# Head pairs taken two by two in the first mixer of a macaron encoder

## The chip, the cores and the metric

The kernel runs on one core of a Trainium2 chip. Its engines work side by side, each through its own queue in order: TensorE (PE) multiplies and transposes into PSUM, ScalarE (ACT) copies and exponentiates, VectorE (DVE) adds, subtracts and normalises, GpSimd (POOL) and SyncE (SP) start loads. They meet through semaphores: an instruction waits until a counter has reached a number. The metric is the device time of one call in microseconds (us).

## The reference

Two layers of 256 frames and width 1024, all in float32. Each layer is an FFN, a mixer and an FFN, each followed by a layer norm. The first layer's mixer is chunked attention with a learned bias by distance; with 256 frames every query sees all keys up to the end of its 64-frame chunk.

```python
for i in range(DEPTH):                                   # DEPTH = 2
    h = swiglu(x, ffn_w_gate[i, 0], ffn_w_up[i, 0], ffn_w_down[i, 0])
    x = layer_norm(ALPHA * x + 0.5 * h, ln_g[i, 0], ln_b[i, 0])
    y = chunked_rel_attention(...) if i % 2 == 0 else stick_breaking_attention(...)
    x = layer_norm(ALPHA * x + y, ln_g[i, 1], ln_b[i, 1])
    h = swiglu(x, ffn_w_gate[i, 1], ffn_w_up[i, 1], ffn_w_down[i, 1])
    x = layer_norm(ALPHA * x + 0.5 * h, ln_g[i, 2], ln_b[i, 2])

# chunked_rel_attention, per 64-frame chunk; 16 heads of 64
qkv = x @ w_qkv
s = einsum('bqhd,bkhd->bhqk', q_c, k_c) * scale + bias
p = softmax(where(valid, s, -inf))
out = einsum('bhqk,bkhd->bqhd', p, v_c)
return out @ w_o
```

## The kernel before

Weights stream from memory in units of 128 x 2048 numbers (1 MB). Each is split into a high and a low part: ACT rounds it (`hi_unit`, L651) and DVE subtracts (`lo_unit`, L847). A product in near-float32 accuracy is then three matmuls, high by high, low by high and high by low (`three`, L344 to L346, 512 columns each). In the query-key blocks and the FFN the weights stand in the array instead, and high and low parts of x run past them in 512 and 256 columns (`qk_block`, L524 and L527).

A mixer has 16 units: four for the values, eight for query and key of a head pair (`qk`), four for the output, a group of two pairs each. Heads go in pairs (`pp` 0 to 7), and a pair passes these steps:

- PE: `qk_block` makes query and key, eight k-steps of four matmuls, in one accumulator `QK` that all pairs share. So the next block waits until the sum of the last one is made (`qk_ready`).
- ACT: `qk_copy` (L754) copies one half of the accumulator to `both`; DVE: `qk_add` (L1029) adds the other and writes `qkT[pp % 2]`, which frees the accumulator.
- PE: `scores` (L564), float32 matmuls of 64 rows, the two heads side by side in the array.
- DVE: `soften` (L994) adds the bias and finds the row's top; ACT: `exps` (L762); DVE: `normalise` (L1001, L1006).
- PE: `turn_probs` (L574), six transposes; ACT: `probsT_copy` (L779) to the one buffer `probsT`.
- PE: `head_out` (L586, L587), float32 matmuls with 64 columns of the array, into `HEADOUT`; ACT: `headout_hi_part` (L783), DVE: `headout_lo_part` (L1033) split the result for the output product.

The order on each engine is written by hand. PE runs pair pp + 1's query-key block, a fill (k-steps of the second value half, or blocks of the output product), pair pp - 1's head products, pair pp + 1's scores and pair pp's transposes, without a stop. ACT and DVE have the splits of units between the steps of a pair (`HI_EARLY`, `HI_LATE`, `LO_EARLY`, `LO_LATE`). The fill `FILL_FIRST` of four k-steps (12 matmuls) stands behind block 0; later fills have two or more. The last output group (g = 3) is the one that needs pairs 6 and 7; its first six matmuls read pair 6, the next pair 7. POOL loads the bias of pair pp + 2 once pair pp is softened. A unit's load starts when the unit four before it has been split.

Of the kernel before, what the change touches and what calls it, by code (L numbers as in the profile page):

```python
# [26 lines left out]
P = 128  # L27
# [42 lines left out]
NORM_SCALE = [(2 * ALPHA, 4 * EPS), (ALPHA, EPS), (2 * ALPHA, 4 * EPS)] * DEPTH  # L70


MIX_ORDER = [("v", 0, 0), ("v", 0, 1), ("qk", 0), ("v", 1, 0), ("qk", 1), ("v", 1, 1), ("qk", 2), ("qk", 3),
             ("qk", 4), ("qk", 5), ("o", 0), ("qk", 6), ("o", 1), ("qk", 7), ("o", 2), ("o", 3)]
# [12 lines left out]
MIX_SLOTS = [0, 1, 4, 2, 3, 0, 4, 1, 3, 4, 1, 3, 2, 0, 3, 4]  # L87
SLOT = (FFN_SLOTS + MIX_SLOTS + FFN_SLOTS) * DEPTH
assert len(SLOT) == UNITS and len(FFN_SLOTS) == UNITS_FFN and len(MIX_SLOTS) == UNITS_MIX
assert sorted(RELEASED) == sorted(MIX_ORDER)  # L90
# [12 lines left out]


# [16 lines left out]
def build(nc, x_in, first_in, units, bias, ln_g, ln_b, table, out):  # L121
    with ExitStack() as ctx:
        def sb(name, shape, dt=F32):
            return ctx.enter_context(nc.sbuf_tensor(name, shape, dt))
# [29 lines left out]
        probs = [in_hT(1, f"probs{p}", [P, 2, KEYS]) for p in range(2)]  # L154
        stick = in_hT(1, "stick", [P, 2, KEYS])
        probsT = in_hT(1, "probsT", [P, 2, KEYS])
        gate_act = sb("gate_act", [P, ROWS, CHUNK_F])
        hidden = sb("hidden", [P, ROWS, CHUNK_F])
        both = sb("both", [P, 2, SEQ])
        hiddenT = sb("hiddenT", [P, SEQ])  # L160
        gain = sb("gain", [P, D])
# [156 lines left out]
        def _(pe):  # L318
# [257 lines left out]

            def head_out(m, pp):
                pe.wait_ge(probsT_done, m * PAIRS + pp + 1)
                if m * PAIRS + pp > 0:
                    pe.wait_ge(headout_lo, m * PAIRS + pp)  # L580
                if pp == GROUPS:
                    pe.wait_ge(v_copied, m * 4 + 4)
                for h in range(2):
                    acc = HEADOUT[h * HD:(h + 1) * HD, :]
                    cols = slice((2 * pp + h) * HD, (2 * pp + h + 1) * HD)
                    pe.matmul(acc, v[:, 0, cols], probsT[:, h, 0:2 * P], start=True, stop=False)  # L586
                    last = pe.matmul(acc[:, P:2 * P], v[:, 1, cols], probsT[:, h, 2 * P:3 * P],  # L587
                                     start=False, stop=True)
                last.then_inc(headout_done, 1)

# [3 lines left out]
                else:  # L594
                    out_half(m, *todo[1:])

            def mixer_matmul(m, t, finish):
                v_block(m, 0, 0, range(KD), t, TURN_BETWEEN)
                transpose_x(t, 1, (2,))
                v_block(m, 0, 1, range(KD), t)  # L600
# [24 lines left out]
                finish((2,))  # L625
# [15 lines left out]
        def _(act):  # L641
# [132 lines left out]

            def probsT_copy(m, pp):
                act.wait_ge(probsT_psum, m * PAIRS + pp + 1)
                if m * PAIRS + pp > 0:
                    act.wait_ge(headout_done, m * PAIRS + pp)
                act.activation(probsT[:], SCORES[pp % 2], ACT.Copy).then_inc(probsT_done, 1)  # L779

            def headout_hi_part(m, pp):
                act.wait_ge(headout_done, m * PAIRS + pp + 1)
                act.activation(hT_hi[:, pp, :], HEADOUT, ACT.Copy).then_inc(headout_hi, 1)  # L783

            def mixer_scalar(m, t):
                n0 = MIX_UNIT[m]
                weights = exps if m % 2 == 0 else sigmoids
                hi_unit(n0 + 2)
                xT_hi_part(t, 1)
                copy_v(m, 0, 0)  # L790
                hi_unit(n0 + 3)
                load_table(ACT.Exp if m % 2 == 0 else ACT.Sigmoid)
                copy_v(m, 0, 1)
                hi_unit(n0 + 4)
                hi_unit(n0 + 5)
                qk_copy(m, 0)
# [16 lines left out]
                        headout_hi_part(m, pp - 1)  # L813
                probsT_copy(m, PAIRS - 1)
                headout_hi_part(m, PAIRS - 1)
                load_table(ACT.Silu)

            def xT_first(piece):
# [25 lines left out]
        def _(dve):  # L844
# [179 lines left out]
            def qk_add(m, pp):  # L1024
# [3 lines left out]
                    dve.wait_ge(scores_done, m * PAIRS + pp - 1)  # L1028
                dve.tensor_tensor(qkT[pp % 2][:], QK[:, :, 0:SEQ], both[:], ALU.add).then_inc(qk_ready, 1)  # L1029

            def headout_lo_part(m, pp):
                dve.wait_ge(headout_hi, m * PAIRS + pp + 1)
                dve.tensor_tensor(hT_lo[:, pp, :], HEADOUT, hT_hi[:, pp, :],  # L1033
                                  ALU.subtract).then_inc(headout_lo, 1)

            def mixer_vector(m, t):
                n0 = MIX_UNIT[m]
                norm(t - 1, 1, split_too=True)
                for n in range(n0 + 2, n0 + 6):
# [153 lines left out]
```

## Time and profile before

| | us |
|---|---|
| median of 3 runs | 977.15 (976.37 to 977.27) |
| the profiled execution | 977.04 |
| its span in the trace | 975.3 |
| PE busy | 963.7 (99%) |
| DVE busy | 644.5 (66%) |
| ACT busy | 487.4 (50%) |
| first mixer in the trace | about 186 to 303 |

The span runs from the first to the last instruction in the trace. TensorE's granted clock over the execution is 0.997 of full speed. PE's durations overlap, since a matmul starts before the last one has left the array; what a matmul costs in a stream is the distance between two starts. A row of the timeline merges equal instructions that follow each other: the start of the first, the time from there to the end of the last, and how many.

### The profile page before, as it was taken

Reading aid. Unit: us, or ns where it says so; the run is one execution under the profiler, and the core shown is the slowest. Engines: PE = TensorE matmul, PEld = TensorE weight load, DVE = VectorE, ACT = ScalarE, POOL = GpSimd, SP = SyncE. Lnnn points to the kernel's source line nnn. Section 1 sums busy time; section 2 is a strip of 40 time slices with the busy share of each in tenths; the row PEclk is TensorE's granted clock in tenths of the full one; section 3 lists DMA queues with packets and bytes.
Section 4 is the critical chain, followed back from the end, with each engine's and each line's share of the span. In section 5 each row is a group of like instructions: output and inputs, shape, how many; then the busy total and the mean of one; then the engine's idle time right before and its main releaser. Section 6 shows DMA issues by size and latency. Waiting matters only on the chain.

```text
span 975.3 us, 13323 instructions
## 1 busy us (share of the span) xinstructions
PE 963.7 (99%) x5184; PEld 810.9 (83%) x5184; DVE 644.5 (66%) x764; ACT 487.4 (50%) x605; POOL 41.5 (4%) x71
## 2 busy tenths in 40 slices
PE   8999999999999999999999999999999999999996
PEld 7888888887878888888888888888878788888885
DVE  6666674777567666664676666638777777666635
ACT  6555562366663555562245555443655445555530
POOL 0200000010101000000000000001112100000000
PEclk9999999999999999999999999999999999999998
DMA  9855556475452755557555555653744445555611
GB/s 355 309 177 194 192 194 244 166 238 180 157 173 96 240 182 185 201 179 253 173 175 190 196 176 200 237 193 129 259 145 154 149 149 197 182 201 178 230 73 44
DMA packets 51116, 183.91 MB, mean 189 GB/s; under 512 B 5856, under 2 KB 6144, under 8 KB 51072
## 3 DMA queue, kind: packets, MB, share of 16 engines
q1 hardware_dynamic: 48368, 175.00, 52.5%
q0 software_dynamic: 2560, 8.18, 2.6%
q8 instruction: 29, 0.48, 0.2%
q10 hardware_dynamic: 144, 0.13, 0.0%
q14 instruction: 15, 0.12, 0.0%
HBM read 182.21 MB, written 1.07 MB: 188 GB/s over the span
## 4 chain that ended last, share of the span: by engine, by line
PE 96%; DMA 1%; DVE 1%; issue 1%; ACT 0%; SPq 0%; POOLq 0%; POOL 0%
PE psum L392 31%; PE psum L396 15%; PE psum L344 12%; PE psum L345 12%; PE psum L346 12%; PE psum L524 6%; PE psum L527 3%; PE psum L564 1%; PE psum L574 1%; DMA raw<-in_units 1%; PE psum L332 1%; PE psum L586 1%; PE psum L587 0%; DVE w_lo L847 0%; SPq L292 0%
## 5 line engine op out<-in xcount | busy, mean ns | idle before, releaser
L847 DVE TENSOR_TENSOR w_lo<-raw,w_hi 128x2048 fp32r<-128x2048 f32 x162 | 369.2, 2291 | 193.9 <-ACT w_hi L651 193.7
L392 PE MATMUL psum<-xT,w_hi 128*128 128x512 f32 x1280 | 402.3, 396 | 0.2 <-DVE both L871 0.2
L651 ACT ACTIVATE w_hi<-raw 128x2048 fp32r<-128x2048 f32 x162 | 307.2, 1908 | 89.7 <-PE psum L346 88.6
L396 PEld LDWEIGHTS psum<-xT,w_lo 128*128 128x128 f32 x1280 | 240.5, 188 | 56.8
L396 PE MATMUL psum<-xT,w_lo 128*128 128x256 f32 x1280 | 251.5, 278 | 0.0
L392 PEld LDWEIGHTS psum<-xT,w_hi 128*128 128x128 f32 x1280 | 195.1, 189 | 0.6 <-DVE both L871 0.4
L344 PE MATMUL psum<-w_hi,hT_hi 128*128 128x512 f32 x416 | 163.3, 393 | 0.0
L345 PE MATMUL psum<-w_lo,hT_hi 128*128 128x512 f32 x416 | 162.0, 389 | 0.0
L346 PE MATMUL psum<-w_hi,hT_lo 128*128 128x512 f32 x416 | 162.0, 389 | 0.0
L694 ACT ACTIVATE hT_hi<-hiddenT 128x256 f32 (+1 forms) x82 | 34.2, 418 | 203.1 <-DVE hiddenT L876 203.1
L346 PEld LDWEIGHTS psum<-w_hi,hT_lo 128*128 128x128 f32 x416 | 78.1, 188 | 16.5
L344 PEld LDWEIGHTS psum<-w_hi,hT_hi 128*128 128x128 f32 x416 | 78.1, 188 | 15.9 <-issue 0.3
L345 PEld LDWEIGHTS psum<-w_lo,hT_hi 128*128 128x128 f32 x416 | 78.2, 188 | 15.3
L524 PE MATMUL psum<-xT,w_hi 128*128 128x512 f32 x256 | 81.5, 399 | 0.0
L881 DVE TENSOR_TENSOR hT_lo<-hiddenT,hT_hi 128x256 f32 (+1 forms) x82 | 34.9, 426 | 54.9 <-ACT hT_hi L694 54.9
L871 DVE TENSOR_TENSOR both<-psum,both 128x512 f32<-128x512 f32 x82 | 56.7, 692 | 8.5 <-ACT both L684 6.8
L527 PEld LDWEIGHTS psum<-xT,w_lo 128*128 128x128 f32 x256 | 48.1, 188 | 11.3
L684 ACT ACTIVATE both<-psum 128x512 f32<-128x512 f32 x82 | 48.9, 596 | 10.7 <-PE psum L396 10.1
L701 ACT ACTIVATE xT<-psum 128x256 fp32r<-128x256 f32 (+1 forms) x30 | 13.1, 455 | 80.2 <-PE psum L332 80.2
L527 PE MATMUL psum<-xT,w_lo 128*128 128x256 f32 x256 | 50.4, 278 | 0.0
L344 PE MATMUL psum<-w_hi,xT 128*128 128x512 f32 x112 | 45.3, 405 | 0.0
L345 PE MATMUL psum<-w_lo,xT 128*128 128x512 f32 x112 | 43.8, 391 | 0.0
(78 smaller groups left out, 642.6 us busy)
## 6 DMA issues: line engine op xcount, KB each, us to landing
raw<-in_units SPq DMA_DIRECT2D x324, 512.0 KB, 4.7
gain<-in_ln_g POOLq DMA_DIRECT2D x6, 512.0 KB, 3.9
shift<-in_ln_b POOLq DMA_DIRECT2D x6, 512.0 KB, 5.0
first<-in_first SPq DMA_DIRECT2D x2, 768.0 KB, 8.8
first<-in_first SPq DMA_DIRECT2D x3, 384.0 KB, 6.2
x<-in_x SPq DMA_DIRECT2D x1, 1024.0 KB, 17.2
rel<-bias_by_distance POOLq DMA_DIRECT2D x8, 128.0 KB, 4.6
out<-x SPq DMA_DIRECT2D x4, 256.0 KB, 2.0
```

The costliest lines, as they stand in the source:

```text
L344: pe.matmul(acc, st[0], mv[0], start=first, stop=False)
L345: pe.matmul(acc, st[0], mv[1], start=False, stop=False)
L346: return pe.matmul(acc, st[1], mv[0], start=False, stop=last)
L392: pe.matmul(TILE[j][:, which, :], as_gu(w_hi[s])[:, k, at:at + P], xT[:, kk, :, :], start=kk == 0, stop=False)
L396: last = pe.matmul(TILE[j][:, which, 0:SEQ], as_gu(w_lo[s])[:, k, at:at + P], xT[:, kk, 0, :], start=False, stop=kk == KD - 1)
L524: pe.matmul(QK[:, which, :], hi[:, k, which * P:(which + 1) * P], xT[:, k, :, :], start=k == 0, stop=False)
L527: last = pe.matmul(QK[:, which, 0:SEQ], lo[:, k, which * P:(which + 1) * P], xT[:, k, 0, :], start=False, stop=k == KD - 1)
L651: act.activation(w_hi[slot][:], raw[raw_slot][:], ACT.Copy).then_inc(hi_done, 1)
L684: act.activation(both[:], TILE[j][:, :, SEQ:], ACT.Copy).then_inc(small_copied, 1)
L847: dve.tensor_tensor(w_lo[slot][:], raw[raw_slot][:], w_hi[slot][:], ALU.subtract).then_inc(lo_done, 1)
L871: dve.tensor_tensor(both[:], TILE[j][:, :, 0:SEQ], both[:], ALU.add).then_inc(summed, 1)
L881: dve.tensor_tensor(hT_lo[:, at, :], hiddenT[:].rearrange("p (k n) -> p k n", k=1), hT_hi[:, at, :], ALU.subtract).then_inc(hT_lo_done, 1)
```

## The change

In the first mixer alone (`DOUBLE = (0,)`) the pairs go two by two. Query-key blocks 2c + 2 and 2c + 3 come with a fill between them, then the transposes of pairs 2c and 2c + 1 together, a fill, the head products of both, and behind these the scores of the next two. The head products of an odd pair have a buffer of their own in PSUM, beside the even pair's, and `probsT` has a second buffer, in the room of the FFN's `gate_act` and `hidden`. High and low parts of two pairs are then made by one 512-column operation on ACT and one on DVE, released for both at once. ACT and DVE follow the same order, written out in `weights_by_two` and `pairs_by_two`. The order of the mixer's weight units and their slots have a table for each mixer; in the first one the last value unit stands one place later and the output units stand behind all query-key units. On DVE the low part of the last unit moves behind the norm. The second mixer keeps its order and its waits, with `probsT` and `HEADOUT` in two buffers.

```diff
+BEFORE_PAIRS = [[("v", 0, (0, 1))], [("v", 0, (2, 3))]]
+BETWEEN_QK = [[("v", 0, (4, 5, 6, 7))], [("v", 1, (3, 4))], [("o", 0, 0, 0)]]
+BEHIND_TURN = [[("v", 1, (0, 1, 2))], [("v", 1, (5, 6, 7))], [("o", 1, 0, 0)]]
+LAST_PAIRS = [[("o", 0, 0, 1), ("o", 0, 1, 0), ("o", 1, 0, 1), ("o", 2, 0, 0)], [("o", 2, 0, 1)], [("o", 0, 1, 1)]]
...
+DOUBLE = (0,)
...
+        probsT = [probsT, nc.alloc_sbuf_tensor_at("probsT1", [P, 2, KEYS], F32, offset=gate_at)]
...
-        HEADOUT = psum[:, 4, 0:SEQ]
+        HEADOUTS = psum[:, 4, :].rearrange("p (k n) -> p k n", k=2)
+        HEADOUT = [psum[:, 4, p * SEQ:(p + 1) * SEQ] for p in range(2)]
...
             def head_out(m, pp):
                 pe.wait_ge(probsT_done, m * PAIRS + pp + 1)
-                if m * PAIRS + pp > 0:
+                if m * PAIRS + pp > 0 and not (m in DOUBLE and pp % 2 == 1):
                     pe.wait_ge(headout_lo, m * PAIRS + pp)
...
+            def pairs_by_two(m):
+                for pp in range(2):
+                    qk_block(m, pp)
+                    for todo in BEFORE_PAIRS[pp]:
+                        fill(m, todo)
+                for pp in range(2):
+                    scores(m, pp)
+                for c in range(PAIRS // 2 - 1):
+                    qk_block(m, 2 * c + 2)
+                    for todo in BETWEEN_QK[c]:
+                        fill(m, todo)
+                    qk_block(m, 2 * c + 3)
+                    for pp in (2 * c, 2 * c + 1):
+                        turn_probs(m, pp)
+                    for todo in BEHIND_TURN[c]:
+                        fill(m, todo)
+                    for pp in (2 * c, 2 * c + 1):
+                        head_out(m, pp)
+                    for pp in (2 * c + 2, 2 * c + 3):
+                        scores(m, pp)
+                for todo in LAST_PAIRS[0]:
+                    fill(m, todo)
+                turn_probs(m, PAIRS - 2)
+                for todo in LAST_PAIRS[1]:
+                    fill(m, todo)
+                turn_probs(m, PAIRS - 1)
+                for todo in LAST_PAIRS[2]:
+                    fill(m, todo)
+                for pp in (PAIRS - 2, PAIRS - 1):
+                    head_out(m, pp)
+
+            def mixer_matmul(m, t, finish):
+                v_block(m, 0, 0, range(KD), t, TURN_BETWEEN)
+                transpose_x(t, 1, (2,))
+                v_block(m, 0, 1, range(KD), t)
+                (pairs_by_two if m in DOUBLE else pairs_by_one)(m)
...
-                if m * PAIRS + pp > 0:
-                    act.wait_ge(headout_done, m * PAIRS + pp)
-                act.activation(probsT[:], SCORES[pp % 2], ACT.Copy).then_inc(probsT_done, 1)
+                if m * PAIRS + pp > 1:
+                    act.wait_ge(headout_done, m * PAIRS + pp - 1)
+                act.activation(probsT[pp % 2][:], SCORES[pp % 2], ACT.Copy).then_inc(probsT_done, 1)
+
+            def headout_hi_two(m, pp):
+                act.wait_ge(headout_done, m * PAIRS + pp + 2)
+                act.activation(hT_hi[:, pp:pp + 2, :], HEADOUTS, ACT.Copy).then_inc(headout_hi, 2)
...
+            def headout_lo_two(m, pp):
+                dve.wait_ge(headout_hi, m * PAIRS + pp + 2)
+                dve.tensor_tensor(hT_lo[:, pp:pp + 2, :], HEADOUTS, hT_hi[:, pp:pp + 2, :],
+                                  ALU.subtract).then_inc(headout_lo, 2)
...
                 norm(t, 0)
+                if m in DOUBLE:
+                    lo_unit(n0 + 17)
```

PE before, from the end of a fill over pair 1's head products to the block behind them (L586 and L587 are `head_out`, L564 `scores`, L574 `turn_probs`, L524 `qk_block`; probsT_56 is the buffer, qkT0 and qkT1 are those of even and odd pairs):

```order
L346 MATMUL psum<-w_hi2,xT 128x512
L586 MATMUL psum<-probsT_56,v_52 64x256
L587 MATMUL psum<-probsT_56,v_52 64x128
L586 MATMUL psum<-probsT_56,v_52 64x256
L587 MATMUL psum<-probsT_56,v_52 64x128
L564 MATMUL psum<-qkT1_51 128x128 x2
L564 MATMUL psum<-qkT1_51 128x256 x2
L574 MATMUL psum<-ident,probs0_53 128x128 x6
L524 MATMUL psum<-xT,w_hi3 128x512 x2
```

PE now, at the first such place (L598 and L599 are `head_out`, L576 `scores`, L536 `qk_block`):

```order
L358 MATMUL psum<-w_hi2,xT 128x512
L598 MATMUL psum<-probsT_56,v_52 64x256
L599 MATMUL psum<-probsT_56,v_52 64x128
L598 MATMUL psum<-probsT_56,v_52 64x256
L599 MATMUL psum<-probsT_56,v_52 64x128
L598 MATMUL psum<-probsT1_57,v_52 64x256
L599 MATMUL psum<-probsT1_57,v_52 64x128
L598 MATMUL psum<-probsT1_57,v_52 64x256
L599 MATMUL psum<-probsT1_57,v_52 64x128
L576 MATMUL psum<-qkT0_50 128x128 x2
L576 MATMUL psum<-qkT0_50 128x256 x2
L576 MATMUL psum<-qkT1_51 128x128 x2
```

Two pairs' head products and two pairs' scores stand together, and no transposes follow them; those (L586 now) stand ahead of a fill.

ACT before, from the copy of the last quarter of the values on (L747 values, L783 high part of head products, L779 `probsT_copy`, L762 `exps`, L651 split, L754 `qk_copy`):

```order
L747 ACTIVATE v_52<-psum 128x512
L783 ACTIVATE hT_hi<-psum 128x256
L779 ACTIVATE probsT_56<-psum 128x768
L762 ACTIVATE probs1_54,total<-probs1_54,neg_top 128x128
L762 ACTIVATE probs1_54,total<-probs1_54,neg_top 128x256
L762 ACTIVATE probs1_54,total<-probs1_54,neg_top 128x128
L762 ACTIVATE probs1_54,total<-probs1_54,neg_top 128x256
L651 ACTIVATE w_hi0<-raw2 128x2048
L754 ACTIVATE both<-psum 128x512
```

ACT now, from the same copy on (L793 values, L697 split, L829 high part of head products, L808 `exps`, L800 `qk_copy` of block 6):

```order
L793 ACTIVATE v_52<-psum 128x512
L697 ACTIVATE w_hi0<-raw0 128x2048
L697 ACTIVATE w_hi1<-raw1 128x2048
L829 ACTIVATE hT_hi<-psum 128x512
L808 ACTIVATE probs0_53,total<-probs0_53,neg_top 128x128
L808 ACTIVATE probs0_53,total<-probs0_53,neg_top 128x256
L808 ACTIVATE probs0_53,total<-probs0_53,neg_top 128x128
L808 ACTIVATE probs0_53,total<-probs0_53,neg_top 128x256
L800 ACTIVATE both<-psum 128x512
```

Two splits of units stand now between the values and the head products' high part, and the copy of the query-key block stands behind one pair's exponentials and ahead of the other's.

DVE before, at the mixer's end (L847 split, L1033 low part of head products, then the norm of the first 128 frames, L904 to L928, and L889, the low part of the transposed x):

```order
L847 TENSOR_TENSOR w_lo0<-raw1,w_hi0 128x2048
L1033 TENSOR_TENSOR hT_lo<-psum,hT_hi 128x256
L847 TENSOR_TENSOR w_lo1<-raw2,w_hi1 128x2048
L1033 TENSOR_TENSOR hT_lo<-psum,hT_hi 128x256
L904 SCALAR_TENSOR_TENSOR x<-x,psum 128x512
L908 BN_STATS stats<-x 128x6
L904 SCALAR_TENSOR_TENSOR x<-x,psum 128x512
```

DVE now, behind the low parts of pairs 6 and 7 (one operation, L1132) and one split: the norm (L1003 to L1027), L946 the split, L988 the low part of the transposed x:

```order
L1003 SCALAR_TENSOR_TENSOR x<-x,psum 128x512
L1007 BN_STATS stats<-x 128x6
L1003 SCALAR_TENSOR_TENSOR x<-x,psum 128x512
L1007 BN_STATS stats<-x 128x6
L1011 BN_AGGR mean_var<-stats 128x2
L1013 TENSOR_SCALAR var_eps<-mean_var 128x1
L1019 SCALAR_TENSOR_TENSOR x<-x,mean_var,gain 128x256 x2
L1027 SCALAR_TENSOR_TENSOR x<-x,rstd,shift 128x256 x2
L1019 SCALAR_TENSOR_TENSOR x<-x,mean_var,gain 128x512
L1027 SCALAR_TENSOR_TENSOR x<-x,rstd,shift 128x512
L946 TENSOR_TENSOR w_lo1<-raw2,w_hi1 128x2048
L988 TENSOR_TENSOR xT<-psum,xT 128x2x128 x2
```

The split of the last unit (w_lo1) stood between the low parts of pairs 6 and 7, and stands now behind the norm, ahead of the transposed x.

## Rows read from the trace of the kernel before

**Rows 1.** The page, part 4: the chain of waits by engine and line.
```profile
PE 96%; DMA 1%; DVE 1%; issue 1%; ACT 0%; SPq 0%; POOLq 0%; POOL 0%
```

**Rows 2.** Timeline of PE (start us, us, engine line op out<-in), values blocks.
```profile
199.75 0.40 PE L344 MATMUL psum<-w_hi,xT 128*128 128x512 f32 x1
204.30 0.39 PE L346 MATMUL psum<-w_hi,xT 128*128 128x512 f32 x1
```

**Rows 3.** Timeline of PE, one visit, from the fill to the next block.
```profile
238.76 0.39 PE L346 MATMUL psum<-w_hi,xT 128*128 128x512 f32 x1
239.07 0.66 PE L586 MATMUL psum<-probsT,v 128*64 128x256 f32 x4
...
241.91 0.28 PE L527 MATMUL psum<-xT,w_lo 128*128 128x256 f32 x1
```

**Rows 4.** Timeline of PE and its weight loads in narrow windows inside that visit.
```profile
239.34 0.39 PE L586 MATMUL psum<-probsT,v 128*64 128x256 f32 x2
...
239.34 0.15 PEld L587 LDWEIGHTS psum<-probsT,v 128*64 128x64 f32 x2
...
239.67 0.29 PE L587 MATMUL psum<-probsT,v 128*64 128x128 f32 x2
...
240.09 0.50 PE L564 MATMUL psum<-qkT 64*128 64x128 f32 x4
...
240.43 0.38 PE L564 MATMUL psum<-qkT 64*128 64x256 f32 x2
...
240.90 0.38 PE L574 MATMUL psum<-ident,probs 128*128 128x128 f32 x2
...
241.34 0.27 PE L574 MATMUL psum<-ident,probs 128*128 128x128 f32 x1
```

**Rows 5.** Timeline of PE, pair 0's scores between two blocks.
```profile
212.60 0.39 PE L346 MATMUL psum<-w_hi,xT 128*128 128x512 f32 x1
...
214.34 0.40 PE L527 MATMUL psum<-xT,w_lo 128*128 128x256 f32 x2
```

**Rows 6.** Timeline of PE behind query-key block 0, and of DVE there.
```profile
210.09 0.40 PE L344 MATMUL psum<-w_hi,xT 128*128 128x512 f32 x1
...
207.16 4.50 DVE L847 TENSOR_TENSOR w_lo<-raw,w_hi 128x2048 fp32r<-128x2048 f32 x2 [2.19 <-ACT w_hi L651]
211.57 0.68 DVE L1029 TENSOR_TENSOR qkT<-psum,both 128x512 f32<-128x512 f32 x1
```

**Rows 7.** Timeline of PE before pair 1's scores.
```profile
220.60 0.39 PE L346 MATMUL psum<-w_hi,xT 128*128 128x512 f32 x1
221.03 0.93 PE L564 MATMUL psum<-qkT 64*128 64x128 f32 x8
```

**Rows 8.** Timelines of PE, ACT and DVE: the sum of query-key block 1.
```profile
219.22 0.39 PE L527 MATMUL psum<-xT,w_lo 128*128 128x256 f32 x2
...
219.65 0.60 ACT L754 ACTIVATE both<-psum 128x512 f32<-128x512 f32 x1 [0.71 <-PE psum L527]
...
220.28 0.69 DVE L1029 TENSOR_TENSOR qkT<-psum,both 128x512 f32<-128x512 f32 x1 [1.90 <-ACT both L754]
```

**Rows 9.** Timelines of DVE and ACT: softening, exponentials and the split behind them.
```profile
214.94 0.28 DVE L994 CUSTOM_DVE_ANT_0 probs<-psum,rel 128x128 f32<-128x128 f32 x1
...
215.26 0.40 ACT L762 ACTIVATE probs<-probs,neg_top 128x128 f32<-128x128 f32 x1 [2.57 <-DVE neg_top L994]
...
217.04 1.90 ACT L651 ACTIVATE w_hi<-raw 128x2048 fp32r<-128x2048 f32 x1
```

**Rows 10.** Timelines of PE and ACT behind the last head products.
```profile
290.92 0.40 PE L587 MATMUL psum<-probsT,v 128*64 128x128 f32 x4
291.25 0.50 PE L344 MATMUL psum<-w_hi,hT_hi 128*128 128x512 f32 x1
...
291.38 0.39 ACT L783 ACTIVATE hT_hi<-psum 128x256 fp32r<-128x256 f32 x1 [1.39 <-PE psum L587]
```

**Rows 11.** Timeline of DVE behind the first norm of the mixer's end.
```profile
301.78 0.76 DVE L889 TENSOR_TENSOR xT<-psum,xT 128x256 fp32r<-128x256 f32 x2 [1.78 <-ACT xT L701]
```

More of the change, by code:

```diff
@@ L86 @@
 FFN_SLOTS = [j % 4 for j in range(24)] + [4, 0, 1, 2, 3, 0, 4, 2, 3]
[L87 to L90, printed above, removed]
+DOUBLE = (0,)
+MIX_SLOTS = [[0, 1, 4, 2, 3, 0, 3, 4, 1, 0, 4, 0, 1, 2, 3, 4], [0, 1, 4, 2, 3, 0, 4, 1, 3, 4, 1, 3, 2, 0, 3, 4]]
+SLOT = [slot for m in range(DEPTH) for part in (FFN_SLOTS, MIX_SLOTS[m], FFN_SLOTS) for slot in part]
+assert len(SLOT) == UNITS and len(FFN_SLOTS) == UNITS_FFN
+assert all(sorted(RELEASED) == sorted(order) and len(order) == UNITS_MIX for order in MIX_ORDERS)
 def mix_unit(m, *unit):
-    return MIX_UNIT[m] + MIX_ORDER.index(unit)
+    return MIX_UNIT[m] + MIX_ORDERS[m].index(unit)
 def uses_done(n):
-    for at in MIX_UNIT:
+    for m, at in enumerate(MIX_UNIT):
         if at <= n < at + UNITS_MIX:
-            return at + RELEASED.index(MIX_ORDER[n - at]) + 1
+            return at + RELEASED.index(MIX_ORDERS[m][n - at]) + 1
     return n + 1
@@ L595, in fill, with pairs_by_one @@
                     out_half(m, *todo[1:])
[L597 to L600, printed above, removed]
+            def pairs_by_one(m):
                 qk_block(m, 0)
@@ L815, in mixer_scalar, with weights_by_two @@
                 headout_hi_part(m, PAIRS - 1)
+            def weights_by_two(m, n0):
+                hi_unit(n0 + 4)
+                hi_unit(n0 + 5)
+                qk_copy(m, 0)
+                qk_copy(m, 1)
+                hi_unit(n0 + 6)
+                hi_unit(n0 + 7)
+                exps(m, 0)
+                qk_copy(m, 2)
+                exps(m, 1)
+                hi_unit(n0 + 8)
+                copy_v(m, 1, 0)
+                hi_unit(n0 + 9)
+                qk_copy(m, 3)
+                probsT_copy(m, 0)
+                probsT_copy(m, 1)
+                hi_unit(n0 + 10)
+                headout_hi_two(m, 0)
+                exps(m, 2)
+                qk_copy(m, 4)
+                exps(m, 3)
+                qk_copy(m, 5)
+                probsT_copy(m, 2)
+                probsT_copy(m, 3)
+                copy_v(m, 1, 1)
+                hi_unit(n0 + 11)
+                hi_unit(n0 + 12)
+                headout_hi_two(m, 2)
+                exps(m, 4)
+                qk_copy(m, 6)
+                exps(m, 5)
+                hi_unit(n0 + 13)
+                hi_unit(n0 + 14)
+                qk_copy(m, 7)
+                probsT_copy(m, 4)
+                probsT_copy(m, 5)
+                hi_unit(n0 + 15)
+                headout_hi_two(m, 4)
+                exps(m, 6)
+                exps(m, 7)
+                probsT_copy(m, 6)
+                probsT_copy(m, 7)
+                hi_unit(n0 + 16)
+                headout_hi_two(m, 6)
+                hi_unit(n0 + 17)
+            def mixer_scalar(m, t):
+                n0 = MIX_UNIT[m]
+                hi_unit(n0 + 2)
+                xT_hi_part(t, 1)
+                copy_v(m, 0, 0)
+                hi_unit(n0 + 3)
+                load_table(ACT.Exp if m % 2 == 0 else ACT.Sigmoid)
+                copy_v(m, 0, 1)
+                (weights_by_two if m in DOUBLE else weights_by_one)(m, n0)
                 load_table(ACT.Silu)
@@ L1059, in mixer_vector, with pairs_by_two @@
                 headout_lo_part(m, PAIRS - 1)
+            def pairs_by_two(m, n0):
+                qk_add(m, 0)
+                qk_add(m, 1)
+                lo_unit(n0 + 6)
+                soften(m, 0)
+                soften(m, 1)
+                lo_unit(n0 + 7)
+                qk_add(m, 2)
+                normalise(m, 0)
+                normalise(m, 1)
+                lo_unit(n0 + 8)
+                lo_unit(n0 + 9)
+                qk_add(m, 3)
+                lo_unit(n0 + 10)
+                headout_lo_two(m, 0)
+                soften(m, 2)
+                soften(m, 3)
+                qk_add(m, 4)
+                normalise(m, 2)
+                normalise(m, 3)
+                qk_add(m, 5)
+                lo_unit(n0 + 11)
+                lo_unit(n0 + 12)
+                headout_lo_two(m, 2)
+                soften(m, 4)
+                soften(m, 5)
+                qk_add(m, 6)
+                normalise(m, 4)
+                normalise(m, 5)
+                lo_unit(n0 + 13)
+                qk_add(m, 7)
+                lo_unit(n0 + 14)
+                soften(m, 6)
+                headout_lo_two(m, 4)
+                soften(m, 7)
+                normalise(m, 6)
+                normalise(m, 7)
+                lo_unit(n0 + 15)
+                headout_lo_two(m, 6)
+                lo_unit(n0 + 16)
+            def mixer_vector(m, t):
+                n0 = MIX_UNIT[m]
+                norm(t - 1, 1, split_too=True)
+                for n in range(n0 + 2, n0 + 6):
+                    lo_unit(n)
+                (pairs_by_two if m in DOUBLE else pairs_by_one)(m, n0)
                 norm(t, 0)
+                if m in DOUBLE:
+                    lo_unit(n0 + 17)
             def xT_first(piece):
@@ L1164, in mixer @@
         made = []
-        for unit in MIX_ORDER:
+        for unit in MIX_ORDERS[m]:
             if unit[0] == "v":
```

30 lines of the change are left out of this document (10 added, 20 removed), and 4 rows, old and new, of the table MIX_ORDERS.

## The prediction

> **What bounds the kernel now.** I read the page's chain of waits first: TensorE (PE) holds 96% of the way to the last instruction [rows 1]. So only what lengthens or shortens PE's own sequence moves the time, and the question is where PE loses time inside the first mixer (roughly 186 to 303 us). For that I read PE's timeline there by start times, because the durations overlap: of matmuls in one stream only the distance from start to start counts.
>
> In the plain stream a 512-column matmul starts every (204.30 - 199.75) / 20 = 0.2275 us [rows 2]. A query-key block lasts from 204.53 (0.23 after the last row of that stream) to 210.09, that is 5.56 us [rows 2, 6]. Call this full-array stream R, the four head products of a pair H (64 columns of the array), its scores S (64 rows), its transposes T. Inside H one 256-column and one 128-column step together take 239.67 - 239.34 = 0.33, so a pair's H costs 0.65; inside S the same two take 240.43 - 240.09 = 0.34, so S costs 0.66 to 0.68 (I take 0.66); transposes follow each other by (241.34 - 240.90) / 4 = 0.11, so T costs 0.65 [rows 4]. These contents stay. What is on top of them are changes from one kind to another [rows 3, 4]:
> - R to H: 0.31 instead of 0.23 up to the first H, then 0.27 instead of 0.22 to the second: 0.13 in all.
> - H to S: 239.67 to 240.09 is 0.42 where two 128-column steps are 0.22: 0.20.
> - S to T: from the last score to the second transpose, 240.43 to 240.90, is 0.47 against 0.22 + 0.11: 0.14; about 0.05 of it lies behind the first T. T to R: 241.34 to 241.91 is 0.57, against 0.11 + 0.46: 0.01 at most.
> - The whole visit R-H-S-T-R, 238.76 to 241.91, is 3.15, contents 0.23 + 0.65 + 0.66 + 0.65 + 0.46 = 2.65: 0.50 on top.
> - R-S-R, 212.60 to 214.34, is 1.74 with contents of 1.35: 0.39 on top [rows 5]. Entering S costs 0.08 + 0.10, so S to R is 0.21.
>
> **The change part by part.** Before, the mixer makes one R-S-R visit (0.39), one R-S-T-R (0.18 + 0.14 + 0.01 = 0.33), six R-H-S-T-R (3.00), one R-H-T-R (0.13 + 0.10 + 0.05 + 0.01 = 0.29) and a last R-H-R. After, there is one R-SS-R (0.39), three times T T inside R (0.06 each: the slow first transpose and the exit) and R-HH-SS-R (0.13 + 0.20 + 0.21 = 0.54), two single T inside R (0.12) and the same last R-H-R, with two pairs in it. That is 4.01 against 0.39 + 1.80 + 0.12 = 2.31: **1.70 saved**. The trace has no H behind H of another pair, no S behind S and no T straight out of R. I take H behind H and S behind S at nothing, as the steps inside a block. Bounds: if each second block pays its entry again without the change of kind (0.05 for four H, 0.10 for four S) the saving is 1.10; if T out of R is free, it is 2.0. Also one wait goes: before pair 1's scores the gap is 0.43 instead of 0.31 [rows 7], 0.12, because only six matmuls stand between the query-key block and its scores; now pair 0's scores stand between too. **Total saved 1.82.**
>
> Here the page TensorEngine Tiling (Array Packing) of the Trainium skill, section Key Properties, has a rule: changing the tiling mode drains TensorE, changing the tile within a mode does not. The trace agrees with it where the kind changes (0.08 to 0.10 before the first matmul), but shows as much again behind it; by the page's part alone 26 changes become 13, about 0.095 each, and the saving would be 1.2 instead of 1.70.
>
> The other side is what the new order puts between a query-key block and the next one. The next block overwrites the accumulator, so it needs the sum of the former (ACT copies, DVE adds). From the last pair of that block's matmuls (219.22) over ACT (219.65) and DVE (220.28) to the released matmul (221.03) it takes 1.81 [rows 7, 8]; ACT to DVE is 0.63, DVE to PE 0.75. Before, the blocks were separated by two fills, scores and transposes or more. Now:
> - **Block 1 behind block 0.** Two k-steps of values stand between, six matmuls, 1.37, so PE is there at 210.09 + 1.37 = 211.46 by the clock of the trace. DVE's sum, which is in the same place of its queue as before (behind two splits of weights), starts at 211.57 and releases 0.75 later, at 212.32 [rows 6]: **0.86**. With DVE free it would be 0.21 (1.81 - 0.23 - 1.37). Behind PE's wait only PE's own blocks stand.
> - **Block 5 behind block 4.** Six matmuls again, queues clear: 1.81 - 0.23 - 1.37 = **0.21**.
> - **Block 7 behind block 6.** Six matmuls of the first output unit. Here ACT and DVE come late, as both units' splits stand ahead. From the last matmul of the second value half (time 0): ACT's copy of values starts at 0.42 (the 512-column matmul's 0.39 and 0.03); an operation overlaps the next by about 0.1 (on DVE 4.50 for two splits whose steps are 4.41 / 2 = 2.205 [rows 6]), so at 0.92 follows the first split of 1.90 [rows 9], done at 2.82; DVE splits two units in 4.41 until 7.26, subtracts the two head products (0.69 less 0.08, as for the same size in [rows 8]), softens; the exponentials start 0.32 behind that (214.94 to 215.26), at 8.19, and the four take 217.04 - 215.26 = 1.78 [rows 9]; then copy and sum, 0.63 + 0.75: 11.35. PE, from the same 0: 0.23 + 0.13 + 1.30 (HH) + 0.20 + 1.32 (SS) + 0.21 + 5.56 + 1.37 = 10.32. **1.03**, with bounds 0.21 (queues clear) and 1.4.
> - Block 3 has twelve matmuls ahead, 2.73 against 1.81 - 0.23: no wait. Blocks 2, 4 and 6 come behind SS, long after their sums.
> - **Output behind the last heads.** The last group needs pair 6's low part, which was made long before; now pairs 6 and 7 are copied and subtracted together behind pair 7's products. From 290.92 ACT starts at 291.38, 0.46 later; then 0.63 and 0.75 for 512 columns, 1.84; PE would be there at 291.25, 0.33 [rows 10]: **1.51**. The six matmuls that covered pair 7's copy before now stand behind it.
> - Four restarts of R with the weights not yet loaded: a weight load with a wait is not drawn ahead. Of the 0.21 from S to R some 0.09 is the change itself (as from R to H), and 0.11 the first weights of R; in pure R the trace has no such restart. I take 0.08 each, 0.3, bounds 0 and 0.45.
> - **Start of the next FFN.** The last weight unit's low split moves behind the first norm on DVE. It takes 2.21 where DVE was idle for 1.78 [rows 11], so the transposed x comes 0.43 later; PE's slack there is small. I take 0.3, bounds 0 and 0.45.
>
> The sum: -1.82 + 0.86 + 0.21 + 1.03 + 1.51 + 0.3 + 0.3 = **+2.39**. The DMA loads keep their number and size; each is started by a split four units earlier, and a late split is what the sum has already. The second mixer keeps its order and its waits; it only gets second buffers that nothing waited for. The profiled execution took 977.04 (span 975.3 and 1.7 around it), 0.1 below the median of 977.15; the forecast is 977.04 + 2.4 = **979.4**.
>
> **Rivals.**
> A, not slower: ACT and DVE aren't behind. If the splits stand elsewhere when PE arrives, the waits of blocks 1 and 7 are the bare chain, 0.21 each, and the FFN's term vanishes: 2.39 - 0.65 - 0.82 - 0.3 = +0.6, 977.6, within the bound. It decides at a block 1 wait of some 0.5. For it: ACT has free time elsewhere, 1.39 before 291.38 [rows 10]; against it: DVE's start at 211.57 is a row, and nothing ahead of it moves.
> B, slower still: the second blocks pay for their weights. A load of weights for array rows in use would have to wait for the running matmul, so HH and SS cost 0.05 and 0.10 more, four times each: +0.6, 980.0. Against it: in H the next weights load from 239.34 while the matmuls of that start run [rows 4], and the step stays 0.22. The rule is in the Trainium skill's page TensorE: Matmul & The Clock Gate, section The mechanism: loads overlap running matmuls only where the row group differs; by that row this trace does not bear it out for H, whose row groups are the same.
> C, faster: the copies are hidden in some way that I don't see, and only the saving stays: 977.04 - 1.82 = 975.2. Against it: 1.51 at the end rests on a semaphore that counts both pairs.
> D, the backlog spreads: ACT's later start at one group delays the next one's transposes, another 1 us or more, 981.
>
> **How the numbers follow.** Forecast 0.60, A 0.17, B 0.12, C 0.05, D 0.06. A measurement of this kernel tells about 0.2%, 1.95 us, from no change. Slower than that: B, D and most of the forecast (its terms must lose 0.45 to miss it), 0.70. Same: 0.23, A and the rest. Faster: 0.07. The range, 977.5 to 980.7, takes in A and B; below it lies C, above it D.
>
> **What would show it.** In the profile after: L586 (transposes), L598 and L576 in three groups of twelve transposes and of doubled H and S, with starts inside HH and SS at the same steps; PE gaps in front of a query-key block (L536) of about 0.9, 0.2 and 1.0 us, and of 1.5 in front of L356 near the mixer's end. I would be wrong if the first of these gaps is missing, if the gap behind the last heads is much under 1 us, or if HH costs more than 1.4.

## The result, and the profile after

The changed kernel takes 979.35 us (979.01 to 980.14, 10 runs); the kernel before, on the same chip, takes 976.75 (976.25 to 977.28, 10 runs). The ratio is 1.0027, 95% interval 1.0018 to 1.0036: slower, by 2.6 us. The forecast was 979.4, which is 2.4 over the 977.04 of the one profiled execution before. The profiled execution has a span of 977.6 against 975.3.

The chain of waits of the page (part 4) is the first thing to read. Against [rows 1] PE has lost 2 points of it; DVE and ACT have one more each:

```profile
PE 94%; DVE 2%; issue 1%; DMA 1%; ACT 1%; SPq 0%; POOLq 0%; POOL 0%; DVEq 0%; ACTq 0%
```

PE's waits (line <- what released it: total, times, longest) name two causes that the kernel before doesn't have, the accumulator's sum (qkT) and the low part of the head products (hT_lo). The list's other rows are waits in the first 21 us of the program. They differ from trace to trace, and block 0 starts between 203.75 and 204.53 in the nine traces here, so I compare PE from query-key block 0 on.

```profile
PE psum L356 <- DVE hT_lo L1132: 1.6, 1, 1.6
PE psum L536 <- DVE qkT L1128: 1.6, 2, 0.8
```

How much the mixer costs is the distance on PE from block 0's first matmul to one matmul behind the mixer that both kernels have, a k-step of the FFN. After, in two windows of PE's timeline:

```profile
204.22 0.62 PE L536 MATMUL psum<-xT,w_hi 128*128 128x512 f32 x2
...
308.48 0.40 PE L357 MATMUL psum<-w_lo,xT 128*128 128x512 f32 x1
```

And before, the same two instructions:

```profile
204.53 0.62 PE L524 MATMUL psum<-xT,w_hi 128*128 128x512 f32 x2
...
306.22 0.40 PE L345 MATMUL psum<-w_lo,xT 128*128 128x512 f32 x1
```

That is 104.26 against 101.69: **the mixer is 2.57 longer**, and from there to the last matmul the distance between the two kernels doesn't change, the second mixer included. The experiments are read by the same distance.

**The visits**, against [rows 3]. PE's timeline around one double group, with the double transposes of another behind it:

```profile
237.87 0.39 PE L358 MATMUL psum<-w_hi,xT 128*128 128x512 f32 x1
238.19 0.66 PE L598 MATMUL psum<-probsT,v 128*64 128x256 f32 x4
238.67 0.40 PE L599 MATMUL psum<-probsT,v 128*64 128x128 f32 x4
238.89 0.65 PE L598 MATMUL psum<-probsT,v 128*64 128x256 f32 x4
239.32 0.44 PE L599 MATMUL psum<-probsT,v 128*64 128x128 f32 x4
239.69 1.58 PE L576 MATMUL psum<-qkT 64*128 64x128 f32 x16
241.20 0.72 PE L536 MATMUL psum<-xT,w_hi 128*128 128x512 f32 x2
241.76 0.40 PE L539 MATMUL psum<-xT,w_lo 128*128 128x256 f32 x2
...
254.20 1.48 PE L586 MATMUL psum<-ident,probs 128*128 128x128 f32 x12
...
255.76 0.40 PE L357 MATMUL psum<-w_lo,xT 128*128 128x512 f32 x1
```

From the last R to the third start of the block it is 241.76 - 237.87 = 3.89, where the prediction's parts give 0.23 + 1.30 + 1.32 + 0.46 + 0.54 = 3.85. The 0.04 sits in the second pair's products: its four 128-column matmuls take 0.44 where the first pair's take 0.40. The twelve transposes and the R behind them take 255.76 - 254.20 = 1.56, and 12 x 0.109 + 0.23 is 1.54: a visit to T alone is nearly free.

**The gaps** before blocks 1, 5 and 7 (against the 0.23 of [rows 2]), behind the last heads (against [rows 10]) and in the FFN:

```profile
210.93 0.39 PE L358 MATMUL psum<-w_hi,xT 128*128 128x512 f32 x1
212.10 0.70 PE L536 MATMUL psum<-xT,w_hi 128*128 128x512 f32 x2 [0.78 <-DVE qkT L1128]
...
248.04 0.39 PE L358 MATMUL psum<-w_hi,xT 128*128 128x512 f32 x1
248.54 0.70 PE L536 MATMUL psum<-xT,w_hi 128*128 128x512 f32 x2
...
267.56 0.39 PE L358 MATMUL psum<-w_hi,hT_lo 128*128 128x512 f32 x1
268.79 0.70 PE L536 MATMUL psum<-xT,w_hi 128*128 128x512 f32 x2 [0.85 <-DVE qkT L1128]
...
291.15 0.44 PE L599 MATMUL psum<-probsT,v 128*64 128x128 f32 x4
293.23 0.47 PE L356 MATMUL psum<-w_hi,hT_hi 128*128 128x512 f32 x1 [1.64 <-DVE hT_lo L1132]
293.53 0.40 PE L357 MATMUL psum<-w_lo,hT_hi 128*128 128x512 f32 x1
...
307.66 0.39 PE L358 MATMUL psum<-w_hi,xT 128*128 128x512 f32 x1
308.17 0.47 PE L356 MATMUL psum<-w_hi,xT 128*128 128x512 f32 x1
```

Note that two of the waits are in no list and carry no bracket. The starts at 248.04 and 307.66 have the next one 0.50 and 0.51 behind them instead of 0.23, but the matmul before is drawn with a modelled length of 0.39, so that the view has only 0.11 and 0.12 of idle time there. By the unrounded starts these waits are 0.28 and 0.29. Behind each wait the second step is 0.31 instead of 0.23 (293.23 to 293.53, 308.17 to 308.48; two merged matmuls read 0.70 instead of 0.62): I call this the restart, 0.08.

Behind the last heads ACT's copy and DVE's subtraction are these:

```profile
291.69 0.60 ACT L829 ACTIVATE hT_hi<-psum 128x512 fp32r<-128x512 f32 x1 [0.34 <-PE psum L599]
...
292.39 0.69 DVE L1132 TENSOR_TENSOR hT_lo<-psum,hT_hi 128x512 fp32r<-128x512 f32 x1 [5.24 <-ACT hT_hi L829]
```

Why block 7's sum is late can be read in ACT's and DVE's timelines (start, duration, engine, line, out<-in, count, idle before):

```profile
257.81 0.60 ACT L793 ACTIVATE v<-psum 128x512 f32<-128x512 f32 x1 [1.24 <-PE psum L358]
258.31 3.71 ACT L697 ACTIVATE w_hi<-raw 128x2048 fp32r<-128x2048 f32 x2
...
265.57 0.40 ACT L808 ACTIVATE probs<-probs,neg_top 128x128 f32<-128x128 f32 x1 [3.08 <-DVE neg_top L1093]
...
267.35 0.58 ACT L800 ACTIVATE both<-psum 128x512 f32<-128x512 f32 x1
```

```profile
260.24 4.49 DVE L946 TENSOR_TENSOR w_lo<-raw,w_hi 128x2048 fp32r<-128x2048 f32 x2 [4.51 <-ACT w_hi L697]
264.65 0.68 DVE L1132 TENSOR_TENSOR hT_lo<-psum,hT_hi 128x512 fp32r<-128x512 f32 x1
...
267.95 0.69 DVE L1128 TENSOR_TENSOR qkT<-psum,both 128x512 f32<-128x512 f32 x1 [0.40 <-ACT both L800]
```

DVE has nothing to split for 4.51 us, since ACT's two splits stand behind the copy of the last quarter of the values (257.81); then come two splits, the subtraction, the softening, the exponentials, and only then the copy that PE is waiting for.

### The profile page after: what moved, and what is told of

Same layout as the page of the kernel before. It is cut to its first block, busy times and chain, and to the rows that moved or that the text cites. A ratio compares the mean times of both kernels' runs of the same rounds, so it can differ in the third digit from the quotient of the medians.

```text
span 977.6 us, 13318 instructions
## 1 busy us (share of the span) xinstructions
PE 963.9 (99%) x5184; PEld 813.3 (83%) x5184; DVE 643.3 (66%) x760; ACT 486.3 (50%) x601; POOL 41.3 (4%) x71
## 4 chain that ended last, share of the span: by engine, by line
PE 94%; DVE 2%; issue 1%; DMA 1%; ACT 1%; SPq 0%; POOLq 0%; POOL 0%; DVEq 0%; ACTq 0%
PE psum L404 31%; PE psum L408 15%; PE psum L356 12%; PE psum L358 12%; PE psum L357 12%; PE psum L536 5%; PE psum L539 3%; PE psum L586 1%; PE psum L576 1%; DMA raw<-in_units 1%; PE psum L344 1%; DVE w_lo L946 1%; PE psum L598 1%; ACT w_hi L697 1%; PE psum L599 0%
## 5 line engine op out<-in xcount | busy, mean ns | idle before, releaser
L946 DVE TENSOR_TENSOR w_lo<-raw,w_hi 128x2048 fp32r<-128x2048 f32 x162 | 369.0, 2290 | 196.4 <-ACT w_hi L697 196.1
L697 ACT ACTIVATE w_hi<-raw 128x2048 fp32r<-128x2048 f32 x162 | 307.0, 1908 | 90.4 <-PE psum L358 88.6
L536 PE MATMUL psum<-xT,w_hi 128*128 128x512 f32 x256 | 81.4, 399 | 1.8 <-DVE qkT L1128 1.6
L747 ACT ACTIVATE xT<-psum 128x256 fp32r<-128x256 f32 (+1 forms) x30 | 13.1, 455 | 80.1 <-PE psum L344 80.1
L356 PE MATMUL psum<-w_hi,xT 128*128 128x512 f32 x112 | 45.5, 407 | 0.1
L358 PE MATMUL psum<-w_hi,xT 128*128 128x512 f32 x112 | 43.8, 391 | 0.0
```

The source lines that it names most:

```text
L356: pe.matmul(acc, st[0], mv[0], start=first, stop=False)
L358: return pe.matmul(acc, st[1], mv[0], start=False, stop=last)
L536: pe.matmul(QK[:, which, :], hi[:, k, which * P:(which + 1) * P], xT[:, k, :, :], start=k == 0, stop=False)
L697: act.activation(w_hi[slot][:], raw[raw_slot][:], ACT.Copy).then_inc(hi_done, 1)
L946: dve.tensor_tensor(w_lo[slot][:], raw[raw_slot][:], w_hi[slot][:], ALU.subtract).then_inc(lo_done, 1)
```

## The experiments

Each kernel is the changed one with one edit, but for the last, which has all that helped. "Mixer" is the distance defined above, against that of the kernel before; the changed kernel has +2.57. The changed kernel's row is that of the result. The other times are medians of 11 runs (5 for the alternating one) beside 27 of the kernel before on the same chip: 976.61 (976.03 to 977.31) for the first four edits, 976.84 (976.25 to 977.49) for the last three.

| kernel | us | ratio to before, 95% | mixer |
|---|---|---|---|
| changed | 979.35 | 1.0027, 1.0018 to 1.0036 | +2.57 |
| a block behind the last heads | 977.73 | 1.0013, 1.0004 to 1.0022 | +1.18 |
| DVE's sum ahead of a split | 978.70 | 1.0022, 1.0013 to 1.0031 | +1.94 |
| ACT's split ahead of a copy | 978.66 | 1.0022, 1.0013 to 1.0031 | +1.83 |
| H S H S instead of H H S S | 979.95 | 1.0035, 1.0021 to 1.0049 | +3.19 |
| last splits ahead of the norm | 978.83 | 1.0021, 1.0012 to 1.0030 | +2.21 |
| one more k-step before block 5 | 978.64 | 1.0021, 1.0012 to 1.0030 | +2.19 |
| all that helped, together | 975.27 | 0.9986, 0.9977 to 0.9995 | -1.16 |

Single terms of 0.3 to 0.7 are near what the timed runs resolve; the trace tells them apart, by gaps that repeat within 0.01 from kernel to kernel. Below, the bare chain is the time of the copy and the sum when neither ACT nor DVE is busy with something else.

### A block behind the last heads

```diff
-LAST_PAIRS = [[... ("o", 2, 0, 0)], [("o", 2, 0, 1)], [("o", 0, 1, 1)]]
+LAST_PAIRS = [[... ("o", 2, 0, 0)], [], [("o", 2, 0, 1)]]
+LAST_COVER = [("o", 0, 1, 1)]      # filled behind the last two head_out
```

> Against the changed kernel (979.35, in its trace 2.57 us more than before from the first mixer on). One output block of six matmuls stands behind the last head products instead of ahead of them. Theory (PE waits 1.7 us there for one copy and one subtraction of both pairs): the wait shrinks by the six matmuls, 1.37, to about 0.3; 978.0, and the wait for hT_lo in front of the last output group goes from 1.6 to 0.2-0.4. Rival (the end of the mixer is bound by what follows, the norm and the transposed x): the time stays at 979.3 and the gap moves to the next FFN's first product.

Measured 977.73, and the mixer 1.39 shorter. PE's timeline at the end of the new cover (lines are up by one here):

```profile
291.70 0.40 PE L359 MATMUL psum<-w_hi,hT_lo 128*128 128x512 f32 x1
292.14 0.47 PE L357 MATMUL psum<-w_hi,hT_hi 128*128 128x512 f32 x1
```

Six matmuls now stand in the gap and 0.21 of it is left (292.14 - 291.70 - 0.23). Nothing turned up later: up to the last matmul the distance to the kernel before grows by 0.01 more. The two `turn_probs` stand together here as well, which by the starts is worth 0.01. So 1.39 of the largest term was the missing cover.

### DVE's sum ahead of a split

```diff
                 qk_add(m, 0)
+                lo_unit(n0 + 5)
                 qk_add(m, 1)
...
-                for n in range(n0 + 2, n0 + 6):
+                for n in range(n0 + 2, n0 + (5 if m in DOUBLE else 6)):
```

> DVE makes the sum of query-key block 0 ahead of the second of the two splits of weights that stand there, instead of behind it. Theory (block 1 waits for DVE's backlog, 0.65 over the bare chain of copy and sum): the gap in front of block 1 falls from 0.94 to about 0.28, the time by 0.65 to 978.7. Rival (the chain itself sets the wait, or the split moved is then late for block 2): the gap stays within 0.2 of 0.94 or turns up in front of block 2; 979.3.

Measured 978.70, the mixer 0.63 shorter. PE in front of block 1, and DVE:

```profile
210.77 0.39 PE L358 MATMUL psum<-w_hi,xT 128*128 128x512 f32 x1
211.30 0.70 PE L536 MATMUL psum<-xT,w_hi 128*128 128x512 f32 x2
```

```profile
210.46 0.69 DVE L1128 TENSOR_TENSOR qkT<-psum,both 128x512 f32<-128x512 f32 x1 [1.47 <-ACT both L800]
```

The gap falls from 1.17 to 0.53: of the extra 0.94, 0.64 was DVE's queue, and 0.30 is the bare chain over six matmuls. The other gaps are as in the changed kernel.

### ACT's split ahead of a copy

```diff
+                hi_unit(n0 + 11)
                 copy_v(m, 1, 1)
-                hi_unit(n0 + 11)
                 hi_unit(n0 + 12)
```

> ACT rounds the unit of query-key block 7 ahead of the copy of the last quarter of the values, instead of behind it; nothing else moves. Theory (block 7 waits since two splits on DVE start only once ACT has made that copy): the gap in front of block 7 falls from 1.01 to the bare chain, about 0.28, as at block 5; 978.6. Rival (it waits since its copy stands behind four exponentials on ACT): the exponentials still stand there, the gap stays over 0.8; 979.3.

Measured 978.66, the mixer 0.74 shorter. PE in front of block 7, and ACT before it:

```profile
267.28 0.39 PE L358 MATMUL psum<-w_hi,hT_lo 128*128 128x512 f32 x1
267.79 0.70 PE L536 MATMUL psum<-xT,w_hi 128*128 128x512 f32 x2
```

```profile
256.18 1.92 ACT L697 ACTIVATE w_hi<-raw 128x2048 fp32r<-128x2048 f32 x1
...
263.55 0.40 ACT L808 ACTIVATE probs<-probs,neg_top 128x128 f32<-128x128 f32 x1 [2.68 <-DVE neg_top L1093]
...
266.32 0.60 ACT L800 ACTIVATE both<-psum 128x512 f32<-128x512 f32 x1 [0.91 <-PE psum L539]
```

The exponentials still stand ahead of the copy, yet the copy now waits for PE (0.91 idle) instead of the reverse, and the extra falls from 1.01 to 0.28. The wait hung on when the two splits began, not on the place of the exponentials: two theories that the changed kernel's trace alone doesn't tell apart.

### H S H S instead of H H S S

```diff
                     for pp in (2 * c, 2 * c + 1):
                         head_out(m, pp)
-                    for pp in (2 * c + 2, 2 * c + 3):
-                        scores(m, pp)
+                        scores(m, pp + 2)
```

> In the three groups, head products of one pair and scores of one pair alternate, H S H S, instead of H H S S: same work, three more changes of kind H to S and three S to H. Theory (each change of kind costs 0.14 to 0.20 on PE): +0.34 for each group, 1.0 in all, less up to 0.35 at block 7, whose wait shrinks when PE comes later; 980.0 to 980.4, the stretch from the first H to the block behind grows from 3.01 to about 3.35. Rival (second blocks pay for their weights anyway, merging brings little): the stretch grows by less than 0.15, 979.4.

Measured 979.95, the mixer 0.62 longer. One group in PE's timeline:

```profile
237.47 0.39 PE L358 MATMUL psum<-w_hi,xT 128*128 128x512 f32 x1
237.79 0.66 PE L598 MATMUL psum<-probsT,v 128*64 128x256 f32 x4
...
238.59 0.93 PE L576 MATMUL psum<-qkT 64*128 64x128 f32 x8
239.45 0.66 PE L598 MATMUL psum<-probsT,v 128*64 128x256 f32 x4
239.93 0.40 PE L599 MATMUL psum<-probsT,v 128*64 128x128 f32 x4
...
241.68 0.40 PE L539 MATMUL psum<-xT,w_lo 128*128 128x256 f32 x2
```

241.68 - 237.47 = 4.21 against 3.89 with the same instructions: 0.32 for two changes of kind more, in each of three groups. The second pair's 128-column matmuls are back at 0.40 (239.93), since they no longer stand behind another pair's, so the 0.04 of that went at the same time: the two changes by themselves are 0.36, 0.18 each. PE comes that much later to block 7, whose wait shrinks from 1.01 to 0.70: 0.96 - 0.31 = 0.65, and 0.62 is measured. This prices a change between head products and scores alone, with no queue in it.

### Last splits ahead of the norm

```diff
+                hi_unit(n0 + 16)
                 probsT_copy(m, 6)
-                hi_unit(n0 + 16)
...
+                lo_unit(n0 + 16)
                 headout_lo_two(m, 6)
-                lo_unit(n0 + 16)
+                lo_unit(n0 + 17)
...
                 norm(t, 0)
-                if m in DOUBLE:
-                    lo_unit(n0 + 17)
```

> The two last weight units are split earlier: ACT rounds the first ahead of pair 6's copy, DVE subtracts it ahead of the last head products' low parts and the last unit ahead of the norm, not behind it. Theory (the last split delays the transposed x, 0.3 in front of the next FFN's second half of k-steps): that gap falls from 0.29 to about 0.03 as before the change, 979.0. Rival (the norm, which starts up to 1 us later now, delays its x and PE with it): a new wait for x of 0.5 or more, 979.6.

Measured 978.83, the mixer 0.36 shorter. The extra 0.29 at 307.66 and its restart are gone from PE (0.22 from start to start, and 0.26 to the next, 308.01), and in front of that place DVE's low part of x starts earlier:

```profile
307.53 0.39 PE L358 MATMUL psum<-w_hi,xT 128*128 128x512 f32 x1
307.75 0.42 PE L356 MATMUL psum<-w_hi,xT 128*128 128x512 f32 x1
```

```profile
303.57 0.76 DVE L988 TENSOR_TENSOR xT<-psum,xT 128x256 fp32r<-128x256 f32 x2 [1.05 <-ACT xT L747]
```

It waits for ACT again, as in [rows 11], and in the changed kernel it stood behind the split until 304.05.

### One more k-step before block 5

```diff
-BETWEEN_QK = [..., [("v", 1, (3, 4))], ...]       BEHIND_TURN = [..., [("v", 1, (5, 6, 7))], ...]
+BETWEEN_QK = [..., [("v", 1, (3, 4, 5))], ...]    BEHIND_TURN = [..., [("v", 1, (6, 7))], ...]
```

> One k-step of values (three matmuls, 0.68) moves from behind the second transposes to between query-key blocks 4 and 5, so nine matmuls stand there instead of six. Theory (block 5 waits for the bare chain of copy and sum, 0.28 with 0.08 of restart behind it): the gap goes, the time falls by 0.36 to 979.0. Rival (six matmuls behind the transposes were needed to cover the copy of the transposed weights): a wait of about 0.3 in front of pair 2's head products takes its place, 979.3.

Measured 978.64, the mixer 0.38 shorter. In PE's timeline no gap is left in front of block 5:

```profile
248.45 0.39 PE L358 MATMUL psum<-w_hi,xT 128*128 128x512 f32 x1
248.67 0.62 PE L536 MATMUL psum<-xT,w_hi 128*128 128x512 f32 x2
```

Three k-steps between two blocks cover the bare chain and two don't; block 7's gap stays at 1.01.

### All that helped, together

```diff
-BEFORE_PAIRS = [[("v", 0, (0, 1))], [("v", 0, (2, 3))]]
+BEFORE_PAIRS = [[("v", 0, (0, 1, 2))], [("v", 0, (3,))]]
-LAST_PAIRS = [[("o",0,0,1), ("o",0,1,0), ("o",1,0,1), ("o",2,0,0)], [("o",2,0,1)], [("o",0,1,1)]]
+LAST_PAIRS = [[("o",0,0,1), ("o",0,1,0), ("o",1,0,1)], [("o",2,0,0)], [("o",0,1,1)]]
+LAST_COVER = [("o",2,0,1)]
```

and the edits of the other kernels but the alternating one.

> Pairs by two with all waits taken out that can be: the moves of the first three experiments (with another output block as the cover), the early splits, the fill at block 5, and three k-steps in front of block 1 and one behind it. Theory (each wait costs what its gap shows and they add): from +2.57 of the first mixer against before, -1.39 -0.63 -0.74 -0.34 -0.36 -0.25 = -1.1; 975.5 against 976.6 of before, what the saved changes of kind (1.8) are worth less one gap of 0.3 in front of block 7 and the slower second heads. Rival (the waits hide each other, the engines' queues are full): -0.3 or less against before, new gaps in front of transposes or head products.

Measured 975.27 (975.05 to 976.01), ratio 0.9986 (0.9977 to 0.9995): the two-by-two order with its covers in place is faster than the kernel before, by 1.6 us; the interval does not reach 1, and the trace gives 1.16 of the 1.6 to the mixer. The chain of waits is PE's again:

```profile
PE 96%; DMA 1%; issue 1%; DVE 1%; SPq 0%; ACT 0%; POOLq 0%; POOL 0%
```

Two short waits are left that the changed kernel had too, 0.28 before block 7 and 0.21 behind the last heads, with their restarts about 0.65 that further cover could give. One is new. Only three matmuls now stand between block 1 and the scores, so pair 1's scores wait for pair 1's sum, and the sixteen score matmuls take 1.72 where they took 1.58 at 239.69 in the changed kernel:

```profile
217.71 1.72 PE L577 MATMUL psum<-qkT 64*128 64x128 f32 x16
```

## Why the prediction was right

The sign, the size and the places came out: +2.57 against +2.39. That the time itself fits to 0.05 (979.35 against 979.4) is in part luck: the sum was 0.18 short, and the 977.04 that it was added to lies 0.29 above the median of ten runs, 976.75. By steps, measured in the trace of the changed kernel:

- **Saved changes of kind**, 1.70 predicted. The waits and restarts sum to 1.03 (block 1) + 0.36 (block 5) + 1.09 (block 7) + 1.67 (output) + 0.34 (FFN) = 4.49; less the 0.12 removed before pair 1's scores and less 2.57, 1.80 is left for the saving. Of the 0.10 more, 0.04 is explained by two terms that were off and nearly cancel: transposes out of R cost 0.02 a visit and not 0.06 (five visits, 0.2 more saved), and a second pair's products cost 0.04 and not nothing (four, 0.16 less). The other 0.06 I give to no step; readings to 0.01 over some ten visits can make as much. The scores' second block costs nothing, as taken. The alternating order prices a change between head products and scores at 0.18 by itself.
- **Block 1**, 0.86 predicted, 0.94 measured; the kernel with DVE's sum ahead of a split says how much of it is queue, 0.64, against 0.86 - 0.21 = 0.65 predicted.
- **Block 5**, 0.21 predicted, 0.28 measured. The bare chain was 0.07 to 0.09 too short in both places (0.30 with DVE free in block 1, 0.28 here and in front of block 7 with ACT's split ahead). The 1.81 of [rows 7, 8] ends at the first matmul of scores; here it is 1.37 + 0.23 + 0.28 = 1.88, or 1.90 by the unrounded starts. The trace shows where the difference lies. ACT's start to DVE's start is 0.63 here as there. But from the start of DVE's sum to the released matmul it is 0.75 in front of scores (220.28 to 221.03) and 0.84 in front of a query-key block (267.95 to 268.79, and 210.46 to 211.30 with DVE's sum ahead), though the sum itself takes 0.69 each time. The prediction took a price paid in front of scores for one paid in front of a full-array stream. Why the latter starts 0.09 later behind its release, no run tests.
- **Block 7**, 1.03 predicted, 1.01 measured, by a chain of seven operations taken from other places of the trace: exponentials 1.78 predicted, 267.35 - 265.57 = 1.78 measured. That it fits to 0.02 is a little luck. Counted from the last matmul of the values, at 257.81 - 0.42 = 257.39, block 7's first matmul came at 11.40 where the sum had 11.35, the 0.09 of the chain being in it, and PE was ready for it at 10.40 where the sum had 10.32.
- **Output behind the last heads**, 1.51 predicted, 1.67 measured. From 291.15 to 293.23 it is 2.08 where [rows 10] have 0.33, 1.75; 0.04 of this lies inside the second pair's products, and the step behind is 0.30 where it was 0.34. The chain from the four 128-column matmuls to the released one is 2.08 against 1.84 predicted, 0.24 longer: to ACT's start 0.54 instead of 0.46 (0.04 of it are the slower products), from ACT to DVE 0.70 instead of 0.63, from DVE to PE 0.84 instead of 0.75, the same 0.09 as above. The cover experiment took 1.39 of the wait back, which shows the cause.
- **Restarts**, 0.3 for four; three of 0.08 were real, and the fourth, behind the last heads, was there before already. The FFN's start, 0.3, was 0.26 and a restart of its own.

The rivals. A (the sums aren't late) falls: the queue ahead of DVE's sum was worth 0.64 and the one ahead of ACT's copy 0.73. B (second blocks pay for their weights) falls in size: 0.04 a second pair of products and nothing for scores, where it said 0.05 and 0.10 for each of four steps. The row-group rule of the Trainium skill's page TensorE: Matmul & The Clock Gate (section The mechanism) is by these rows not what sets the step of H; the same section also lets a load go ahead into a background weight buffer, and these rows can't tell whether that is what happens. The drain on a change of tiling mode in the Trainium skill's page TensorEngine Tiling (Array Packing), Key Properties, agrees in direction with the alternating kernel; the 0.18 a change measured there is a price that this section doesn't give. C falls with the output's 1.67. D had ACT's delay spread from group to group: no gap of the changed kernel stands anywhere that the sum didn't name.

What was tested by an edit is the cause of the waits at blocks 1, 5 and 7, at the output and in the FFN, and the price of a change between head products and scores. The prices of the other changes of kind, the 0.04 of a second pair's products and the 0.09 of the chain are read from traces only, and the 1.80 saved is what is left once the waits are taken off.

## What to carry to other kernels

A change between head products and scores on TensorE costs 0.18 us here, and the thirteen changes that the grouping saves are together worth 1.80, 0.14 each. But what stood between two uses of one accumulator was also the cover of the copies on other engines: before moving it, work out the bare chain (here 1.9 us from the start of the block's last two matmuls, some eight matmuls of 512 columns) and count what is left in between at every use. A late copy is as often the queue in front of it: one swap of a split and a copy that isn't urgent was worth 0.7. When a reordering that saves work comes out slower, mend its waits before it is given up: six moves of neighbouring work turned +2.6 us into -1.6.

## What was not expected of the hardware

- Transposes straight out of R run at 0.109 each from the first on; behind scores the first takes 0.165 (from the trace of the kernel before, 240.74 to 240.90, in the visit of [rows 4]).
- The head products of a second pair behind a first take 0.04 more, though they are the same instructions in the same columns: 0.44 against 0.40 for the four 128-column ones, in all four places. In the trace the matmuls of the pair's two heads start 0.013 apart in the first pair and 0.057 apart in the last six of the second's eight; what sets that distance is open.
- A full-array stream that has waited for a semaphore takes 0.31 instead of 0.23 for its first step, whatever it waited for (DVE's sum at 212.10, 248.54 and 268.79, the head products at 293.23, x at 308.17).
- The start behind the release differs by what is released: 0.15 behind the end of DVE's operation for a full-array matmul (five places: 212.10, 248.54, 268.79 and 293.23 here, 211.30 with DVE's sum ahead), 0.05 for the scores at 221.03 in the kernel before.
